# A hybrid decoder step on one core: the sampled-attention stage in another order, and two output tiles computed in pieces

## Chip, cores and metric

One Trainium2 chip, one core. The metric is device time in microseconds (us) of one execution. The kernel before took 1250.9 us (median of three runs, 1247.67 to 1252.53).

## The reference, cut to what matters

The kernel runs one step of a two-layer decoder for 512 prompt tokens and 8 sampled requests of 4 tokens each (32 sampled tokens), `D_MODEL` 1024. Layer 0 projects its input, runs a causal convolution on one half (LayerNorm, then `silu`) and attention with a forget gate on the other, and multiplies the concatenation with `w_out`. The sampled tokens attend to 256 cached rows in pages of 128, found by a page table, and to their own new rows:

```
y = jax.nn.silu(layer_norm(out, ln_g, ln_b))                      # conv branch
k_all = jnp.concatenate([gather_pages(cache_k[e], page_table), k], axis=1)
v_all = jnp.concatenate([gather_pages(cache_v[e], page_table), v], axis=1)
att = fox_attend(q, k_all, v_all, f_all[:, past_len:], f_all, q_pos_s, k_pos_s)
merged = jnp.concatenate([a_out, att.reshape(*att.shape[:2], D_B)], axis=-1)
xs = xs + merged @ wo
```

A squared-ReLU MLP (hidden 4096) follows in each layer; layer 1 has a spatial-gating unit in the place of attention.

## The kernel before, in words

Activations lie feature-major: `xT[128, 8, 544]`, tokens in the columns (32 sampled, then 512 prompt), 8 blocks of 128 features. Every dense product is made from three fp32r products: operands are split into a high part (ScalarE, `_hi`) and the rest (VectorE, `_lo`), and TensorE adds hi·hi, lo·hi and hi·lo into PSUM (`ps`, 8 banks of 512). One output tile (`tile`, L789) is 8 blocks k × 3 products × 2 halves of 272 columns, 48 matmuls, into a pair of banks. Weights come in blocks of 256 columns through `w_raw` (SyncE's queue) and are split by `split_hi` and `split_lo`.

Each engine has its own instruction list, written out by hand and joined by semaphores; an engine works strictly in its own order. Around the change, in layer 0:

- **Prompt attention** runs through 32 items (head, query block): scores and transposed probabilities on TensorE, maximum and normalisation on VectorE, exponent on ScalarE. The convolution's taps fill VectorE between them; the LayerNorm's variance is summed by TensorE (`channel_sums`, L999) after item 30. `pair_hi`/`pair_lo` write the attention result into `A_hi`/`A_lo`, blocks 4 to 7.
- **Sampled stage.** For each of 8 requests, `turn_pages(b)` (L1074) transposes the two pages of keys, 8 transposes into two banks; ScalarE copies one bank and VectorE the other to `kc_T` (`page_copy`). A slot of `kc_T` is used again by request b+4, so the copies of requests 4 to 7 wait for the first four requests' scores. `sample_scores(g)` for a group of four requests first adds the terms that need no page (forget sums, mask, own keys; L1087 to L1094), then the 32 products with the pages (L1100). Then `sample_max`, `sample_exp`, `sample_share`, `turn_sample` (three transposes), `sample_copy`, `sample_new_values` (L1123), `sample_values` (L1133), `own_heads`, `turn_values` (L1141), `gather_heads` (L2113), `sampled_lo`, which writes the 32 sampled columns of `A_hi`/`A_lo`, blocks 4 to 7.
- In the same stretch ScalarE takes the LayerNorm's square root, VectorE inverts it in four quarters (L2088) and scales `c_f` (L2090), ScalarE applies `Silu` (L1574) and rounds to `A_hi`, blocks 0 to 3 (L1579), VectorE writes `A_lo` (L2126) and splits the first three output tiles' weights (L1804). The `Silu` part stands after both groups' scores, since `q_bd`, `kn_T`, `nf_T` and `self_q` lie in the bytes of `A_hi`, blocks 0 to 3.
- **Output projection:** eight tiles (L800). Tile j is added to `xT` by VectorE (`add_to_x`, L2135); then ScalarE and VectorE prepare that block as an operand of the MLP (`to_ffn`): a series of roundings and subtractions per tile, the split of the next weights, sums of squares, and from the third tile on the weight sums of the first products of the MLP. Tile j+2 may start when tile j has been added.
- **MLP:** blocks are multiplied by a seven-product scheme in the order `ORDER` (L1213). The first six products of a chunk are p1, p5, p1, p5, p2, p2; the next, p6, waits for `part_11` (L2253), a reduction by VectorE.
- **Queues.** SyncE issues, in order: keys of requests 0 to 2, values of 0 to 3, keys of 3 to 7 (from request 5 on each after the transposes of request b-5), values of 4 to 7 (after the transposes of requests 3, 4, 6, 7), then the last two blocks of `w_out`, then the MLP's weights. GpSimd loads `w_spatial` and `b_spatial` after the first output tile.

Of the kernel before, what the change touches and what calls it, by code (L numbers as in the profile page):

```python
# [24 lines left out]
F32 = mybir.dt.float32  # L25
# [59 lines left out]
def build(nc, i, o):  # L85
# [78 lines left out]
    with ExitStack() as ctx:  # L164
# [104 lines left out]
        q_bd = at("q_bd", [P, PAIRS, NB, HQ], F32, reg1)  # L269
        kn_T = at("kn_T", [P, PAIRS, NS], F32, reg1 + 4096)  # L270
        nf_T = at("nf_T", [H * NB, KS], F32, reg1 + 4608)
        self_q = at("self_q", [H * NB, 2, P], F32, reg1 + 5760)
        assert 6784 <= CT * TB
        kc_T = [at(f"kc_T{s}", [P, PAIRS, NEWC], F32, reg2 + 4096 * s) for s in range(4)]
# [50 lines left out]
        MIX_BANK, MIX_BANK_S = (2, 4, 5), (3, 6, 7)  # L325
        X_BANK = (0, 2, 6)
# [307 lines left out]
        def _(pool):  # L634
# [103 lines left out]
            pool.memset(q_bd[:, :, :, :], 0.0).then_inc(bd_zero, 1)  # L738
# [50 lines left out]
        def _(pe):  # L789
            def tile(j, n, hi, lo, first_waits=None, k0=0, kn=KT):  # L790
# [3 lines left out]
                s = j % 2  # L794
# [283 lines left out]
            def sample_scores(g):  # L1078
# [14 lines left out]
                for p2 in range(PAIRS):  # L1093
                    pe.matmul(out[:, NEWC:KS], q_bd[:, p2, 4 * g:4 * g + 4, :].rearrange("p b c -> p (b c)"), kn_T[:, p2, :],  # L1094
                              start=False, stop=False, skip_group_check=True)
                for g_ in range(PAGES):
                    pe.wait_ge(kcT_evac[g_], 4 * g + 4)
                for p2 in range(PAIRS):
                    for b4 in range(4):
                        mm = pe.matmul(out[HQ * b4:HQ * b4 + HQ, 0:NEWC], q_bd[:, p2, 4 * g + b4, :],  # L1100
                                       kc_T[b4][:, p2, :], start=False, stop=(p2 == PAIRS - 1), skip_group_check=True)
                mm.then_inc(sc_done, 1)

            def turn_sample(g):
                pe.wait_ge(sp_ready, g + 1)
                out = ps[:, 2, :]
                if g == 0:
                    pe.wait_ge(kcT_evac[0], NB)
# [6 lines left out]
            def sample_new_values(g):  # L1115

                pe.wait_ge(spT_evac, g + 1)
                if g == 0:
                    for g_ in range(PAGES):
                        pe.wait_ge(kcT_evac[g_], NB)  # L1120
                else:
                    pe.wait_ge(root_done, 1)
                pe.matmul(ps[:, 5 + g, :], p_sT[0:NS, g, 2, :], v_nat[0:NS, 0, :], start=True, stop=False,  # L1123
                          skip_group_check=True)

            def sample_values(g):
# [3 lines left out]
                for u in range(PAGES):  # L1130
                    for b4 in range(4):
                        c = HQ * b4
                        mm = pe.matmul(ps[c:c + HQ, 5 + g, :], p_sT[:, g, u, c:c + HQ], v_pg[4 * g + b4][:, u, :],  # L1133
# [3 lines left out]
            def turn_values(g):  # L1137

                pe.wait_ge(own_done, g + 1)
                for p2 in range(PAIRS):  # L1140
                    mm = pe.transpose(ps[:, 3 + g, P * p2:P * p2 + P], own[:, g, P * p2:P * p2 + P], ident[:, :])  # L1141
# [12 lines left out]
            sample_new_values(1)  # L1154
            sample_values(1)
            turn_values(0)


            def merged_ready(k):
                if k == 2:  # L1160
                    turn_values(1)
                if k < CT:
                    pe.wait_ge(cyo_done, k + 1)
                else:
                    pe.wait_ge(ml_done, PAIRS + 2)

            pe.wait_ge(spT_evac, 2)
            for j in range(8):
                tile(j, N_OUT + j, A_hi, A_lo, merged_ready if j == 0 else None)
# [160 lines left out]
        def _(act):  # L1330
# [144 lines left out]
            def sample_prep(h):  # L1475

                rows_ = slice(HD * (h % 2), HD * (h % 2) + HD)
                act.activation(q_bd[rows_, h // 2, :, NQ * h:NQ * h + NQ],
# [46 lines left out]
            for s in range(FIRST_ALONE, H * QT):  # L1525
                item_slot(s)
                if 12 <= s < 12 + H:
                    if s == 12:
                        act.wait_ge(bd_zero, 1)
                    sample_prep(s - 12)  # L1530
# [907 lines left out]
```

## Time and profile before

| | |
|---|---|
| median of three runs | 1250.9 us |
| profiled execution, its own time | 1246.93 us |
| its span in the trace | 1245.2 us |
| busy: TensorE / VectorE / ScalarE / GpSimd | 96% / 69% / 49% / 5% |
| chain that ended last: TensorE / VectorE / ScalarE | 86% / 7% / 3% |
| granted TensorE clock, mean | 0.99 |

The profiled execution's time stands 1.73 us above its span. Busy shares are of the whole span; the stage at hand is some 40 us of it, from 250 to 290 us. A window view gives busy time per stretch, a timeline the instructions in order with the idle time before each and what ended it. The granted clock (PEclk) is a share of full speed: 1.00 stands for 2.4 GHz, 0.50 for 1.2 GHz.

### The profile page before, as it was taken

The page shows a single profiled execution, that of the slowest core. Times are in us where ns is not written, and L with a number is a line of the kernel's source. Part 1 is how long each engine was busy: PE and PEld are TensorE (multiplying, and loading weights), DVE is VectorE, ACT ScalarE, POOL GpSimd, SP SyncE. Part 2 cuts the span into 40 slices and gives each one's busy share as a digit, 9 for nine tenths or more (in the row PEclk, how much of TensorE's full clock was granted, in tenths as well). Part 3 has the DMA queues.
Part 4 walks back from the last instruction along what each step waited for, and adds up shares of the span by engine and source line. Part 5 has one row for each costly group of instructions (what it writes and reads, how often), then busy time and mean ns, then how long its engine had stood idle before and what let it go on. Part 6 is the DMA issues. An engine that isn't in the chain of part 4 may idle for free.

```text
span 1245.2 us, 23181 instructions
## 1 busy us (share of the span) xinstructions
PE 1199.5 (96%) x9394; PEld 1158.6 (93%) x9394; DVE 856.1 (69%) x1416; ACT 604.3 (49%) x1174; POOL 64.9 (5%) x111
## 2 busy tenths in 40 slices
PE   6999998889999999999999999989999999999998
PEld 5999886658999999999999999989999999999998
DVE  5798888656895685684686635678965855856852
ACT  5636644634564264273374424635652652642641
POOL 4010300000000000000000031030000000000000
PEclk9999997989999999999999999999999999999999
DMA  5431321344134143143142123222241251341312
GB/s 160 105 99 57 90 99 37 102 153 136 35 100 138 34 137 102 38 158 109 41 132 68 44 93 102 68 73 69 68 157 47 70 169 35 101 137 35 131 40 73
DMA packets 111777, 113.41 MB, mean 91 GB/s; under 512 B 6430, under 2 KB 105898, under 8 KB 111663
## 3 DMA queue, kind: packets, MB, share of 16 engines
q1 hardware_dynamic: 110111, 107.50, 26.7%
q0 software_dynamic: 1472, 4.41, 1.1%
q8 instruction: 75, 1.23, 0.4%
q14 instruction: 31, 0.25, 0.1%
q10 hardware_dynamic: 88, 0.02, 0.0%
HBM read 107.18 MB, written 5.16 MB: 90 GB/s over the span
## 4 chain that ended last, share of the span: by engine, by line
PE 86%; DVE 7%; ACT 3%; issue 2%; DMA 1%; POOL 1%; SPq 0%; ACTq 0%; DVEq 0%
PE ps L1237 31%; PE ps L1213 26%; PE ps L800 18%; PE ps L1039 5%; PE ps L952 1%; DMA w_raw<-in_w_in_ab 1%; DVE c_f L1893 1%; PE ps L982 1%; PE ps L999 1%; POOL A_lo L774 1%; PE ps L964 1%; DVE a_f L2411 1%; DVE w_lo L2174 1%; DVE w_lo L1804 0%; PE ps L1100 0%
## 5 line engine op out<-in xcount | busy, mean ns | idle before, releaser
L1597 ACT ACTIVATE w_hi<-w_raw 128x512 fp32r<-128x512 f32 x320 | 197.5, 626 | 236.8 <-PE ps L1237 177.7
L2174 DVE TENSOR_TENSOR w_lo<-w_raw,w_hi 128x512 fp32r<-128x512 f32 x320 | 214.3, 684 | 11.0 <-ACT w_hi L1597 10.9
L1237 PE MATMUL ps<-A_hi,w_hi 128*128 128x272 f32 x1024 | 212.4, 289 | 0.0
L1237 PE MATMUL ps<-A_lo,w_hi 128*128 128x272 f32 x1024 | 212.1, 289 | 0.0
L1237 PE MATMUL ps<-A_hi,w_lo 128*128 128x272 f32 x1024 | 211.3, 288 | 0.0
L1237 PEld LDWEIGHTS ps<-A_hi,w_hi 128*128 128x128 f32 x1024 | 161.0, 188 | 0.1
L1237 PEld LDWEIGHTS ps<-A_hi,w_lo 128*128 128x128 f32 x1024 | 161.0, 189 | 0.0
L2333 DVE TENSOR_TENSOR t_f<-ps,r_all 128x544 f32<-128x544 f32 x64 | 46.3, 724 | 166.3 <-PE ps L1237 166.3
L1237 PEld LDWEIGHTS ps<-A_lo,w_hi 128*128 128x128 f32 x1024 | 159.9, 189 | 0.0
L1213 PE MATMUL ps<-B_lo,w_hi 128*128 128x272 f32 x512 | 147.8, 289 | 0.0
L1213 PE MATMUL ps<-B_hi,w_lo 128*128 128x272 f32 x512 | 147.6, 288 | 0.0
L1213 PE MATMUL ps<-B_hi,w_hi 128*128 128x272 f32 x512 | 147.5, 288 | 0.0
L1213 PE MATMUL ps<-t_h,w_hi 128*128 128x272 f32 x384 | 111.7, 291 | 3.4 <-DVE w_lo L2174 3.4
L1213 PE MATMUL ps<-t_l,w_hi 128*128 128x272 f32 x384 | 111.3, 290 | 0.0
L1213 PE MATMUL ps<-t_h,w_lo 128*128 128x272 f32 x384 | 110.6, 288 | 0.0
L1213 PEld LDWEIGHTS ps<-B_hi,w_lo 128*128 128x128 f32 x512 | 96.5, 188 | 0.0
L1213 PEld LDWEIGHTS ps<-B_hi,w_hi 128*128 128x128 f32 x512 | 96.5, 188 | 0.0
L1213 PEld LDWEIGHTS ps<-B_lo,w_hi 128*128 128x128 f32 x512 | 96.4, 188 | 0.0
L800 PE MATMUL ps<-A_hi,w_hi 128*128 128x272 f32 x384 | 81.7, 294 | 8.2 <-DVE xT L1836 3.9
L1893 DVE SCALAR_TENSOR_TENSOR c_f<-glu_p,conv_wT,c_f 128x512 f32<-128x512 f32 x120 | 83.4, 741 | 0.2
L800 PE MATMUL ps<-A_lo,w_hi 128*128 128x272 f32 x384 | 80.6, 292 | 0.0
L800 PE MATMUL ps<-A_hi,w_lo 128*128 128x272 f32 x384 | 80.4, 291 | 0.0
(328 smaller groups left out, 2417.3 us busy)
## 6 DMA issues: line engine op xcount, KB each, us to landing
w_raw<-in_w_ff_up SPq DMA_DIRECT2D x64, 512.0 KB, 4.7
w_raw<-in_w_ff_down SPq DMA_DIRECT2D x64, 512.0 KB, 5.3
w_raw<-in_w_in_ab SPq DMA_DIRECT2D x20, 512.0 KB, 4.7
w_raw<-in_w_in_c SPq DMA_DIRECT2D x16, 512.0 KB, 4.4
w_raw<-in_w_out_ab SPq DMA_DIRECT2D x8, 512.0 KB, 4.8
k_pg<-in_cache_k SPq DMA_DIRECT2D x16, 256.0 KB, 4.6
v_pg<-in_cache_v SPq DMA_DIRECT2D x16, 256.0 KB, 3.8
w_raw<-in_w_out_c SPq DMA_DIRECT2D x8, 512.0 KB, 4.4
```

The lines of the kernel that those rows point to most:

```text
L774: pool.tensor_tensor(A_lo[:, k, :], a_f[:, k % 2, :], A_hi[:, k, :].bitcast(F32), ALU.subtract)\
L800: mm = pe.matmul(ps[:, 2 * s + half, 0:HALF], wt[:, j % 4, k, :], mv[:, k, half * HALF:(half + 1) * HALF], start=(k == 0 and at_ == 0), st ...
L952: pe.matmul(ps[:, bank, 0:n], qT[0:HD + 2, h, NS + P * q:NS + P * q + P], kT[0:HD + 2, h, NS:NS + n], start=True, stop=False, skip_group_c ...
L964: mm = pe.transpose(ps[:, 4 + s % 2, P * j:P * j + P], prob[:, s % 3, P * j:P * j + P], ident[:, :])
L982: mm = pe.matmul(ps[HD * even:HD * even + HD, 7, P * q:P * q + P], v_nat[:, 1 + j, HD * h:HD * h + HD], pT[(2 * t + even) % 6][:, P * j:P ...
L1039: mm = pe.matmul(nat_ps(m), mv[:, k, c0:c0 + P], wt[:, s:s + 2, k, :], start=(k == 0 and at_ == 0), stop=(k == KT - 1 and at_ == 2))
L1213: mm = pe.matmul(ps[:, product_bank((name, u)), 0:HALF], wt[:, k, :], mv[:, k, :], start=(name in ("p1", "p2", "p5") and k == 0 and at_ == 0),
L1237: mm = pe.matmul(down_banks(u)[:, half, :], wt[:, k % KH, :], mv[:, k, half * HALF:(half + 1) * HALF], start=(k == 0 and at_ == 0), stop=( ...
L1597: act.activation(ring(w_hi, q), half_source(q), ACT.Copy).then_inc(fh_done, 1)
L1893: dve.scalar_tensor_tensor(out=c_f[:, c, NS:T], in0=glu_p[:, c, tap:tap + S], scalar=conv_wT[:, c, tap:tap + 1], in1=c_f[:, c, NS:T], op0= ...
L2174: dve.tensor_tensor(ring(w_lo, q), half_source(q), ring(w_hi, q).bitcast(F32), ALU.subtract)\
L2333: dve.tensor_tensor(two(t1_f[:, 1, :]), down_banks(j), two(r_all[:, :]), ALU.mult).then_inc(dn_evac, 1)
```

## The change

On TensorE, `sample_scores` becomes `sample_biases` (the terms without pages) and `sample_keys`; the biases are placed between pages, the keys of group 0 after page 4. Output tiles 0 and 1 are cut into `out_part` pieces and placed between the steps of the sampled values; the half of columns 272 to 543 (without sampled tokens) is closed first. Bank pairs of the eight tiles follow `OUT_PAIR`; the other PSUM banks move with them (turned probabilities to 7, sampled values to 4 and 5, turned values to 6 and 7). `q_bd` moves into the prompt columns of `qT`, heads 0 and 1, and `self_q`, `nf_T`, `kn_T` into `nat_buf`, so `A_hi` is free earlier; `kc_T` is moved accordingly. GpSimd's clearing of `q_bd` waits for the scores of heads 0 and 1 too, VectorE's `forget_rows` (at item 10) for the stores of keys, ScalarE's `sample_prep` (from item 12 on) for `forget_rows`.

```diff
TensorE
-            for b in range(6):
-                turn_pages(b)
-            sample_scores(0)
+            def out_part(j, ks, halves):
+                n = N_OUT + j
+                if ks[0] == 0:
+                    pe.wait_ge(lo_done, n + 1)
+                    if j == 0:
+                        pe.wait_ge(kcT_evac[0], NB)
+                    else:
+                        pe.wait_ge(sexp_done, 2)
+                for k in ks:
+                    if k < CT:
+                        pe.wait_ge(cyo_done, k + 1)
+                    else:
+                        pe.wait_ge(ml_done, PAIRS + 2 if 0 in halves else PAIRS)
...
+            turn_pages(0)
+            turn_pages(1)
+            sample_biases(0)
+            turn_pages(2)
+            turn_pages(3)
+            sample_biases(1)
+            turn_pages(4)
+            sample_keys(0)
+            turn_pages(5)
             turn_pages(6)
             turn_pages(7)
-            sample_scores(1)
+            sample_keys(1)
+            out_part(0, range(0, CT), (0, 1))
             turn_sample(0)
+            out_part(0, range(CT, KT), (1,))
+            turn_sample(1)
             sample_new_values(0)
             sample_values(0)
-            turn_sample(1)
             sample_new_values(1)
             sample_values(1)
+            out_part(1, range(0, 1), (0, 1))
             turn_values(0)
...
+            out_part(1, range(1, 3), (0, 1))
+            turn_values(1)
+            out_part(1, range(3, CT), (0, 1))
+            out_part(1, range(CT, KT), (1,))
+            out_part(0, range(CT, KT), (0,))
+            out_part(1, range(CT, KT), (0,))
+            pe.wait_ge(ats_ok, 2)
+            for j in range(2, 8):
+                tile(j, N_OUT + j, A_hi, A_lo)
ScalarE
+                if s == H * QT - 2:
+                    act.activation(soft[:, 3, 0:1], eps[:, 0:1], ACT.Sqrt)
+            act.wait_ge(var_done, 1)
+            act.activation(two(r_all[:, :]), ps[:, 0:2, 0:HALF], ACT.Sqrt, bias=eps[:, 1:2], scale=1.0 / DA)\
+               .then_inc(root_done, 1)
             pair_hi(PAIRS - 1)
...
+            page_copy(0)
+            page_copy(1)
+            act.activation(soft[:, 3, 1:2], eps[:, 0:1], ACT.Silu)
+            page_copy(2)
+            page_copy(3)
+            smooth(0)
+            smooth(1)
+            for b in range(4, NB):
+                page_copy(b)
+            smooth(2)
+            smooth(3)
+            sample_exp(0)
+            sample_exp(1)
+            sample_copy(0)
+            sample_copy(1)
VectorE
+            for n in range(N_OUT, N_OUT + 3):
+                split_lo(n, n)
+            dve.wait_ge(root_done, 1)
+            link(dve.reciprocal(r_all[:, 0:T // 4], r_all[:, 0:T // 4]))
             pair_lo(PAIRS - 1)
...
+            for b in range(4):
                 page_copy(b)
...
+                if b < 3:
+                    invert_quarter(b + 1)
+            for c in range(CT):
+                dve.tensor_tensor(c_f[:, c, :], c_f[:, c, :], r_all[:, :], ALU.mult).then_inc(normed, 1)
+            page_copy(4)
+            page_copy(5)
+            smooth_lo(0)
+            page_copy(6)
+            smooth_lo(1)
+            page_copy(7)
+            sample_max(0)
+            smooth_lo(2)
             sample_max(1)
+            smooth_lo(3)
+            sample_share(0)
             sample_share(1)
```

`smooth(c)` is the `Silu` and the rounding of block c, `smooth_lo(c)` its rest; before, the three splits, the quarters and the scalings stood between the page copies, and `A_lo` of blocks 0 to 3 after `own_heads(0)`.

## Rows read from the trace of the kernel before

**Rows 1.** Windows: busy us of PE, PEld, DVE, ACT, POOL, PEclk, DMA, GB/s

```profile
250.44:260.15 9.71, 6.21 (x51) 5.15 (x49) 8.19 (x10) 4.76 (x7) 0.00 (x0) 1.00 0.70 239
260.15:267.73 7.58, 7.49 (x50) 4.93 (x49) 1.49 (x2) 0.00 (x0) 0.00 (x0) 0.55 0.11 43
267.73:289.59 21.86, 17.61 (x140) 10.85 (x140) 14.10 (x32) 12.82 (x24) 0.00 (x0) 1.00 0.30 97
289.59:343.90 54.31, 54.31 (x432) 54.23 (x432) 43.45 (x78) 28.82 (x53) 2.47 (x7) 1.00 0.29 98
343.90:345.74 1.84, 0.14 (x3) 0.03 (x1) 1.84 (x4) 0.63 (x1) 0.00 (x0) 1.00 0.00 0
```

**Rows 2.** Timeline of TensorE: start, length, operation, count, [idle before, releaser]

```profile
252.02 1.94 PE L1074 MATMUL ps<-ident,k_pg 128*128 128x128 f32 x16 [0.49 <-DVE A_lo L1989]
...
271.11 0.75 PE L1087 MATMUL ps<-nf_T,sel 64*128 64x288 f32 x2
...
273.55 1.93 PE L1100 MATMUL ps<-kc_T,q_bd 128*32 128x256 f32 x32
...
276.67 1.12 PE L1123 MATMUL ps<-v_nat,p_sT 32*128 32x512 f32 x2 [0.70 <-ACT p_sT L1553]
...
279.57 0.33 PE L1111 MATMUL ps<-ident,prob_s 128*128 128x128 f32 x1
```

**Rows 3.** Operations of VectorE, 250.4 to 289.6: count, busy us, mean ns, idle

```profile
L2076 DVE COPY kc_T<-ps 128x512 f32<-128x512 f32 x8 | 5.5, 684 | 6.8 <-PE ps L1100 6.1 <-PE ps L1074 0.7
...
L1804 DVE TENSOR_TENSOR w_lo<-w_raw,w_hi 128x1024 fp32r<-128x1024 f32 x4 | 4.9, 1224 | 0.1
...
L2088 DVE RECIPROCAL r_all<-r_all 128x136 f32<-128x136 f32 x4 | 4.0, 995 | 0.1
...
L2126 DVE TENSOR_TENSOR A_lo<-c_f,A_hi 128x544 fp32r<-128x544 f32 x4 | 2.9, 724 | 3.0 <-ACT A_hi L1579 3.0
...
L2113 DVE TENSOR_REDUCE at_s<-ps 128x16 f32<-128x128 f32 x8 | 1.8, 281 | 0.0
```

**Rows 4.** Timeline of ScalarE in the sampled stage

```profile
268.87 1.28 ACT L1547 ACT_TABLE_LOAD   x1
...
281.14 0.82 ACT L1574 ACTIVATE c_f<-c_f,vec 128x544 f32<-128x544 f32 x1
```

**Rows 5.** Timelines of GpSimd and VectorE: last store of keys, `self_q`

```profile
159.22 0.75 POOL L725 DMA_DIRECT2D out_k_prompt<-nat_buf  x1 [2.30 <-DVE nat_buf L1969]
...
205.33 0.47 DVE L2000 TENSOR_TENSOR self_q<-ps,sel 64x128 f32<-64x128 f32 x2
```

**Rows 6.** The page's DMA issues: count, KB each, us to landing

```profile
k_pg<-in_cache_k SPq DMA_DIRECT2D x16, 256.0 KB, 4.6
```

**Rows 7.** Timeline of VectorE: the additions to `xT`, and the first reduction

```profile
292.90 0.72 DVE L2135 TENSOR_TENSOR xT<-ps,xT 128x544 f32<-128x544 f32 x1 [2.23 <-PE ps L800]
...
298.91 0.72 DVE L2135 TENSOR_TENSOR xT<-ps,xT 128x544 f32<-128x544 f32 x1 [0.52 <-PE ps L800]
...
304.92 0.72 DVE L2135 TENSOR_TENSOR xT<-ps,xT 128x544 f32<-128x544 f32 x1 [0.62 <-PE ps L800]
...
316.95 0.72 DVE L2135 TENSOR_TENSOR xT<-ps,xT 128x544 f32<-128x544 f32 x1 [0.37 <-PE ps L800]
...
328.98 0.72 DVE L2135 TENSOR_TENSOR xT<-ps,xT 128x544 f32<-128x544 f32 x1 [0.24 <-PE ps L800]
...
344.92 0.71 DVE L2253 TENSOR_REDUCE t_f<-ps 128x272 f32<-128x544 f32 x1
```

**Rows 8.** Timeline of TensorE: the restart in the first feed-forward layer

```profile
345.74 0.36 PE L1213 MATMUL ps<-t_h,w_hi 128*128 128x272 f32 x1 [1.70 <-DVE w_lo L2174]
```

**Rows 9.** Timeline of TensorE near the kernel's start

```profile
22.04 0.82 PE L800 MATMUL ps<-A_hi,w_hi 128*128 128x272 f32 x2 [3.87 <-DVE xT L1836]
...
25.30 0.41 PE L800 MATMUL ps<-A_hi,w_lo 128*128 128x272 f32 x2
```

**Rows 10.** A stretch of the attention stage, columns as in rows 1

```profile
202.70:216.30 13.60, 10.86 (x47) 6.57 (x45) 11.15 (x29) 6.28 (x22) 0.00 (x0) 0.50 0.01 4
```

More of the change, by code:

```diff
@@ L268, in build @@
         gate = at("gate", [H, 4, T], F32, zone_kT + 12288)
[L269 to L274, printed above, removed]
+        q_all = at("q_all", [P, 2, T], F32, reg2)
+        q_bd = [q_all[:, p2 // 2, NS + NB * HQ * (p2 % 2):NS + NB * HQ * (p2 % 2) + NB * HQ].rearrange("p (b c) -> p b c", b=NB)
+                for p2 in range(PAIRS)]
+        self_q = at("self_q", [H * NB, 2, P], F32, zone_nb)
+        nf_T = at("nf_T", [H * NB, KS], F32, zone_nb + 1024)
+        kn_T = at("kn_T", [P, PAIRS, NS], F32, zone_nb + 2176)
+        assert 2688 <= 3 * 4 * 4 * (HD + 2) and 2 * TB <= 5120
+        kc_T = [at(f"kc_T{s}", [P, PAIRS, NEWC], F32, reg2 + (4096 * s + 5120 if s < 3 else 2 * KT * TB - 6144))
+                for s in range(4)]
         K_SLOTS = (zone_t, zone_t + 4096, zone_gs, zone_glu, zone_glu + 4096)
@@ L1117, in sample_new_values @@
                 pe.wait_ge(spT_evac, g + 1)
[L1118 to L1123, printed above, removed]
+                pe.wait_ge(kcT_evac[1], NB - 1 + g)
+                pe.matmul(ps[:, 4 + g, :], p_sT[0:NS, g, 2, :], v_nat[0:NS, 0, :], start=True, stop=False,
                           skip_group_check=True)
@@ L1139, in turn_values @@
                 pe.wait_ge(own_done, g + 1)
+                if g == 1:
+                    pe.wait_ge(spT_evac, 2)
                 for p2 in range(PAIRS):
-                    mm = pe.transpose(ps[:, 3 + g, P * p2:P * p2 + P], own[:, g, P * p2:P * p2 + P], ident[:, :])
+                    mm = pe.transpose(ps[:, 6 + g, P * p2:P * p2 + P], own[:, g, P * p2:P * p2 + P], ident[:, :])
                 mm.then_inc(own_T, 1)
-            for b in range(6):
-                turn_pages(b)
-            sample_scores(0)
+            def out_part(j, ks, halves):
[11 more added lines that the diff above has]
+                        pe.wait_ge(ml_done, PAIRS + 2 if 0 in halves else PAIRS)
+                    for wt, mv, at_ in ((w_hi, A_hi, 0), (w_lo, A_hi, 1), (w_hi, A_lo, 2)):
+                        for half in halves:
+                            mm = pe.matmul(ps[:, 2 * OUT_PAIR[j] + half, 0:HALF], wt[:, j % 4, k, :],
+                                           mv[:, k, half * HALF:(half + 1) * HALF],
+                                           start=(k == 0 and at_ == 0), stop=(k == KT - 1 and at_ == 2),
+                                           skip_group_check=True)
+                if ks[-1] == KT - 1 and 0 in halves:
+                    mm.then_inc(tile_done, 1)
@@ L2123, in _ @@
             own_heads(0)
-            for c in range(CT):
-                dve.wait_ge(cyh_done, c + 1)
-                dve.tensor_tensor(A_lo[:, c, :], c_f[:, c, :], A_hi[:, c, :].bitcast(F32), ALU.subtract).then_inc(cyo_done, 1)
             own_heads(1)
```

90 lines of the change are left out of this document (30 added, 60 removed).

## The prediction

> **What bounds the kernel now.** I began with the busy shares: TensorE has 96% of the span, so time can only be won where it waits, and where it runs at half clock. The table of windows [rows 1] shows where. From 250.44 to 260.15 us it is busy for 6.21 of 9.71 us; from 260.15 to 267.73 it is busy, but at a granted clock of 0.55; from 267.73 to 289.59 it stands still for 4.25 us more. Then 432 matmuls follow in 54.31 us without a gap, 0.126 us each. One more gap comes after them, 1.84 us before 345.74, in which VectorE is busy all the time. So there are two places: the sampled stage, and the entry to the MLP.
>
> The timeline of TensorE gives the stage's prices at full clock [rows 2]: 16 transposes in 1.94 us, so 0.11 us each and 0.9 us per request; the terms without pages from 271.11 to 273.55, 2.44 us; 32 products with pages 1.9 us; new and cached values of a group from 276.67 to 279.57, 2.90 us. Three turned pieces cost 0.4 us at the transposes' pace, a block of an output tile 6 × 0.126 = 0.75 us [rows 1]. The first group did the same terms and products in the window at 0.55, in 7.58 us in place of 4.35: half clock cost 3.2 us [rows 1, 2].
>
> The second view is VectorE's timeline after the stage [rows 7]. Between its first addition at 292.90 and the end of the reduction at 345.63 it waits for TensorE only four times: 0.52, 0.62, 0.37 and 0.24 us, 1.75 us in all. So the 52.7 us are a chain of VectorE's (with ScalarE's roundings in it), not of TensorE's. The product p6 needs that reduction, and TensorE's restart at 345.74 is that wait [rows 8] (the row names the split just before, which stands on the same list).
>
> **The stage, step by step.** Page 1 still starts at 252.02, after `A_lo` [rows 2]. What is put before it is covered: the square root and its table load fall in ScalarE's wait for the last probabilities, the three splits and one quarter of the inverse in VectorE's wait for `pair_hi`. Uncovered, they would put on the path about 2 us of ScalarE (a load of 1.28 us and a root priced like a `Silu`, 0.82 us [rows 4]) or 4.7 us of VectorE (three splits of 1.22 and a quarter of 1.00 [rows 3]).
>
> TensorE's new list, at the prices above: page 1 to 252.9; terms of group 0 to 255.4; pages 2 and 3 to 257.2; terms of group 1 to 259.65; page 4 to 260.55; products of group 0 to 262.4; pages 5 to 7 to 265.1. The terms cover the copies on which the pages used to wait. VectorE's four copies, three quarters and four scalings of c, 8.6 us at most at 0.68, 1.00 and 0.72 us (the last from the rests, which have the scalings' shape [rows 3]), fit between 251.9 and 261.4. From 262.4 it makes four copies and two rests of 0.72 us, with hardly a wait: the last copy ends at about 266.7, and TensorE waits 1.6 us. Products of group 1 to 268.7; four blocks of tile 0 to 271.7.
>
> Under them runs what used to stand on the path: ScalarE ends the fourth `Silu` (0.82 us [rows 4], its rounding counted the same at most) at 268.4, loads the `Exp` table (1.28 us [rows 4]) and has both exponents by 270.9. VectorE's shares are ready by then. So: turned probabilities 0 to 272.1, four half blocks (12 matmuls, 1.5 us) to 273.6, turned probabilities 1 to 274.0, values of both groups to 279.8. One block, turned values 0, two blocks, turned values 1, one block, with 0.45 us for each turning: 283.7. Half of tile 1 to 285.2, tile 0's other half to 286.7. The sampled columns go through VectorE and ScalarE meanwhile, four reductions of 0.28 us per group [rows 3], a rounding and a rest of 64 columns, under 1.6 us. The second group's start at 283 and are ready by 284.6, 0.6 us before they are needed; without that cover, 3 us of them would stand on the path.
>
> Tile 0 is added at about 287.0 in place of 292.90, and tile 1 is complete at 288.3, about 10.5 us earlier than now. In terms: 7.8 us of waits before 289.59, less 2.1 that stay (0.5 and 1.6), 3.2 us of half clock, and 1.6 us for the drain of the last matmul before each of some ten waits, which the records count as busy.
>
> **What reaches the end.** TensorE is 10.5 us ahead, but VectorE's chain begins only with tile 0, 5.9 us earlier, and it needs its 52.7 us less the 1.75 us of waits that now fall away [rows 7]: 287.0 + 51.0 + 0.1 = 338.1, against 345.74. **The gain at the restart is 7.6 us**, and behind it TensorE has no gap in which to lose it. TensorE, six products past its tiles, gets there at 333.5: its gap grows from 1.7 to about 4.5 us. What is late next is thus VectorE's list.
>
> A longer gap has a price that rows of the same kind show. After a gap of 3.87 us at the kernel's start, dense matmuls go at half pace: seven pairs from 22.04 to 25.30 take 3.26 us, where seven at 0.25 take 1.75, so 1.5 us lost [rows 9]. The gap of 1.70 us cost nothing: the clock stayed at 1.00 [rows 1, 8]. A gap of 4.5 is nearer to the first, so I take 1.5; the ends are 0 and the 3.2 us above. The Trainium skill, page "TensorE: Matmul & The Clock Gate", section "HAM oscillation — how this bites in real kernels", says that a long idle stretch between bursts sends the engine back to half rate. By that rule the gain is 6.1, by the row of the short gap alone 7.6.
>
> **Edits with no price of their own.** The bank moves change no instruction. VectorE's wait for stored keys at item 10 has scores and ScalarE's exponents behind it, but the last store was issued at 159.22, and `self_q` is written at 205.33 [rows 5]. ScalarE's wait at item 12 adds nothing: its exponent of item 14, ahead of it, already depends on `self_q` through item 14's scores. GpSimd's clearing of `q_bd` waits for eight items' scores, which TensorE issues before the projections that it waited for already. SyncE's gathers follow the transposes: request 7's keys are issued 2.5 us later, at 256.5, and land by the median of 4.6 us [rows 6] at 261 to 262, before 264.2; values 5 come later too, values 6 and 7 and the third weight block about 5 us earlier, at 264 to 266.5, 10 us before use. The fourth weight block, the MLP's first block and GpSimd's two loads move forward 4 to 6 us together, as close to one another as now. Were a key page late after all, every us would go onto the path.
>
> **Sum.** The profiled execution took 1246.93 us: 1246.93 - 7.6 + 1.5 = 1240.8. The median of the runs is 0.32% above that execution; in its measure the forecast is 1244.8 us. About 0.5%, 6.3 us, can be told from no change here.
>
> **Rivals.**
> - *The clock holds at the gap.* For it: the short gap; against it: rows 9. Gain 7.6, 1243.3 us.
> - *The clock falls among the pages as well.* In 250.44 to 260.15 TensorE did nothing but transposes and waits, at 1.00, and only then fell [rows 1]. The new order mixes in matmuls, but has its longest wait, 1.6 us, behind three pages of transposes. Price 3.2 us on the path: gain 2.9, 1248.0 us. The Trainium skill's same page, section "Part 4: PE-mode transpose", says that transposes do not count as busy for the clock. By that rule this is the likelier case; the trace, with 9.7 us of them at 1.00, agrees in part at best.
> - *TensorE's lead is kept whole.* VectorE's chain would have to be shorter than its rows, by hidden waits in it: gain 10.5 less 1.5 at most, up to 10.5 without the drop, 1240.4 us. Against it: VectorE's full windows before 345.74.
> - *Slower: the clock falls among the pages and stays down.* In the attention stage it stayed at 0.50 for 13.6 us [rows 10], with work as sparse as the sampled one. Here it would cost half of that, 6.8, and the later drop 1.5: 8.3 against 7.6, 0.7 us slower, 1251.6 us. It turns slower from 12.2 us at half clock on; over the whole stage, 31 us, it would be near 1260.
> - *The early table loads do not do what they are for*: `Silu`'s load stands on the path again, 1.28 us [rows 4]. Gain 4.8, 1246.1 us.
>
> **How the numbers follow.** Forecast 0.47; clock holds 0.20; clock falls among the pages 0.13; lead kept 0.08; slower 0.06; table loads 0.06. The forecast's gain of 6.1 lies at the edge of 0.5%; its unknowns (0 to 3.2 for the drop, about 1 us for the start of the chain) split it evenly. Faster: half of the forecast, nearly all of the clock that holds, the lead kept: 0.47. Slower by over 0.5% is the long half clock alone: 0.03. The rest, 0.50, lies within. The range goes from the lead kept, 1240, to the fall among the pages with the runs' own scatter, 1249; only the slower case and parts of the outer ones lie outside.
>
> **What would show it.** Right: page 7's copy is the only long wait in 252 to 288; the first addition to `xT` at about 287; four waits of VectorE gone from the additions; a gap of 4 to 5 us on TensorE that ends about 7.6 us earlier than 345.74 with `part_11`; then a granted clock of 0.5 for about 3 us. Wrong: a clock under 1.00 between 255 and 285, a wait of a page for its gather, a first addition later than 289, or an MLP that starts over 9 us earlier.

## The result and the profile after

| | before | after |
|---|---|---|
| median of the runs | 1248.56 us (8 runs, 1246.22 to 1252.53) | 1242.02 us (8 runs, 1237.76 to 1243.86) |
| ratio after to before | | 0.9943, 95% interval 0.9928 to 0.9958 |
| profiled execution: time, span | 1246.93, 1245.2 us | 1243.86, 1242.2 us |
| page 0 to the first addition to `xT` | 42.46 us | 36.66 us |
| page 0 to product p6 | 95.30 us | 87.41 us |
| gap of TensorE ahead of p6, first layer | 1.70 us | 4.08 us |
| p6 to the first finished block (`d0`) | 42.85 us | 44.37 us |

The change makes the kernel 6.5 us faster by the medians, 0.57%; forecast were 6.1 us. A second set of runs of the same kernel gave 1240.53 us and a ratio of 0.9935 (0.9914 to 0.9955).

The two profiled spans differ by only 3.0 us, because the profiled execution of after comes to page 0 at 253.89 us in place of 250.44. These 3.45 us arise ahead of page 0 and not in the sampled stage: the first scores of the prompt attention are already 1.45 us late (165.74 against 164.29 us), and in the attention stage TensorE's clock is lower for longer (mean granted clock from 195 to 235 us 0.79 against 0.83). Over all executions profiled in this study, of either kernel and its variants, page 0 starts between 248.9 and 253.9 us. So the stages are compared from page 0 on, and never by the spans.

First the table of windows of after, with stretches that answer to [rows 1]: page 0 to the score terms, to the first piece of tile 0, to the last piece, to the last product ahead of p6, the gap, and what follows it.

```profile
core 0: us, PE busy (x) PEld busy (x) DVE busy (x) ACT busy (x) POOL busy (x), PEclk, DMA share, GB/s
253.89:263.60 9.71, 9.15 (x74) 8.25 (x73) 7.92 (x12) 5.07 (x8) 0.00 (x0) 1.00 0.57 163
263.60:272.17 8.57, 7.01 (x93) 4.88 (x91) 6.12 (x11) 7.72 (x13) 0.00 (x0) 1.00 0.71 232
272.17:291.87 19.70, 19.70 (x151) 15.08 (x148) 7.53 (x20) 4.11 (x12) 0.75 (x1) 1.00 0.26 86
291.87:337.20 45.33, 45.33 (x362) 45.12 (x360) 39.03 (x72) 27.26 (x52) 1.72 (x7) 1.00 0.31 106
337.20:341.30 4.10, 0.01 (x1) 0.03 (x1) 4.10 (x8) 1.53 (x3) 0.00 (x0) 1.00 0.00 0
341.30:345.00 3.70, 3.70 (x18) 3.70 (x19) 2.40 (x5) 0.91 (x2) 0.00 (x0) 0.57 0.55 177
```

From 253.89 to 337.20 us the granted clock is 1.00 throughout, where [rows 1] had 0.55 for 7.58 us. TensorE is busy for 16.16 of the first 18.28 us, and from 272.17 on it makes 513 matmuls in 65 us without a gap. Then it stands still for 4.10 us in which VectorE is busy all the time, and the 3.70 us behind that go at 0.57. From here to the end, half clock costs 1.5 us more than before (p6 to `d0`: 44.37 against 42.85).

The timeline of TensorE through the stage:

```profile
255.54 1.06 PE L1079 MATMUL ps<-ident,k_pg 128*128 128x128 f32 x8 [0.56 <-DVE A_lo L2028]
...
270.31 1.93 PE L1109 MATMUL ps<-kc_T,q_all 128*32 128x256 f32 x32 [1.56 <-DVE kc_T L2121]
...
272.17 0.52 PE L1165 MATMUL ps<-A_hi,w_hi 128*128 128x272 f32 x2
...
275.27 0.27 PE L1118 MATMUL ps<-ident,prob_s 128*128 128x128 f32 x1
```

These answer to [rows 2]. Page 1 waits as it did. The only long wait among pages is that of group 1's products for page 7's copy, 1.56 us. The first piece of tile 0 starts 1.86 us later, and from there on no row has an idle time in front.

VectorE's additions and its first reduction, which answer to [rows 7], and TensorE's restart, [rows 8]:

```profile
290.55 0.72 DVE L2184 TENSOR_TENSOR xT<-ps,xT 128x544 f32<-128x544 f32 x1 [1.20 <-PE ps L1165]
...
295.96 0.72 DVE L2184 TENSOR_TENSOR xT<-ps,xT 128x544 f32<-128x544 f32 x1
...
301.27 0.72 DVE L2184 TENSOR_TENSOR xT<-ps,xT 128x544 f32<-128x544 f32 x1
...
312.83 0.72 DVE L2184 TENSOR_TENSOR xT<-ps,xT 128x544 f32<-128x544 f32 x1
...
324.54 0.72 DVE L2184 TENSOR_TENSOR xT<-ps,xT 128x544 f32<-128x544 f32 x1
...
331.24 0.72 DVE L2184 TENSOR_TENSOR xT<-ps,xT 128x544 f32<-128x544 f32 x1
...
340.47 0.72 DVE L2302 TENSOR_REDUCE t_f<-ps 128x272 f32<-128x544 f32 x1
```

```profile
341.30 0.36 PE L1246 MATMUL ps<-t_h,w_hi 128*128 128x272 f32 x1 [4.08 <-DVE w_lo L2223]
```

The first addition waits for TensorE; no later one does. From 290.55 to the end of the reduction VectorE takes 50.64 us, against 52.7 before. The longer gap ahead of p6 is what the change leaves to TensorE: it is early, and VectorE's list is not.

### The profile page after: what moved, and what is told of

The parts are those of the page before. It is cut to its first block, busy times and chain, and to the rows that moved or that the text cites. A ratio compares the mean times of both kernels' runs of the same rounds, so it can differ in the third digit from the quotient of the medians.

```text
span 1242.2 us, 23180 instructions
## 1 busy us (share of the span) xinstructions
PE 1199.2 (97%) x9394; PEld 1160.6 (93%) x9394; DVE 855.9 (69%) x1416; ACT 605.3 (49%) x1176; POOL 64.9 (5%) x111
## 4 chain that ended last, share of the span: by engine, by line
PE 85%; DVE 8%; ACT 3%; issue 1%; DMA 1%; POOL 1%; SPq 0%; ACTq 0%; DVEq 0%
PE ps L1270 31%; PE ps L1246 26%; PE ps L805 15%; PE ps L1044 5%; PE ps L957 1%; DMA w_raw<-in_w_in_ab 1%; PE ps L1165 1%; DVE w_lo L1843 1%; PE ps L987 1%; DVE c_f L1932 1%; DVE w_lo L2223 1%; PE ps L1004 1%; PE ps L969 1%; POOL A_lo L779 1%; DVE a_f L2460 1%
## 5 line engine op out<-in xcount | busy, mean ns | idle before, releaser
L1270 PE MATMUL ps<-A_hi,w_hi 128*128 128x272 f32 x1024 | 212.2, 288 | 0.0
L1270 PE MATMUL ps<-A_lo,w_hi 128*128 128x272 f32 x1024 | 212.0, 288 | 0.0
L1270 PE MATMUL ps<-A_hi,w_lo 128*128 128x272 f32 x1024 | 211.2, 288 | 0.0
L805 PE MATMUL ps<-A_hi,w_hi 128*128 128x272 f32 x352 | 75.4, 296 | 8.2 <-DVE xT L1875 4.3
L1246 PEld LDWEIGHTS ps<-t_h,w_hi 128*128 128x128 f32 x384 | 73.0, 190 | 6.3 <-DVE w_lo L2223 6.2
L805 PE MATMUL ps<-A_lo,w_hi 128*128 128x272 f32 x352 | 74.1, 292 | 0.0
```

The costliest lines, as they stand in the source:

```text
L805: mm = pe.matmul(ps[:, 2 * s + half, 0:HALF], wt[:, j % 4, k, :], mv[:, k, half * HALF:(half + 1) * HALF], start=(k == 0 and at_ == 0), st ...
L1246: mm = pe.matmul(ps[:, product_bank((name, u)), 0:HALF], wt[:, k, :], mv[:, k, :], start=(name in ("p1", "p2", "p5") and k == 0 and at_ == 0),
L1270: mm = pe.matmul(down_banks(u)[:, half, :], wt[:, k % KH, :], mv[:, k, half * HALF:(half + 1) * HALF], start=(k == 0 and at_ == 0), stop=( ...
```

## The experiments

All profiles were read in the same three stretches, so that the early part of an execution does not enter. Page 0 is TensorE's first transpose of a key page, the first addition is VectorE's first `add_to_x`, and `d0` stands for the first finished block of the feed-forward layer, read at the start of VectorE's first addition `xT<-t_f,xT`. The runs were made in sets, each beside its own runs of the kernel before: their median was 1249.92 us beside `after_5`, `early_sums`, `fill_gap` and `tile0_only`, and 1247.30 us beside the others. So across sets the ratios are compared, not the medians.

| kernel | page 0 to first addition | page 0 to p6 | p6 to `d0` | median, us | ratio to before, 95% |
|---|---|---|---|---|---|
| before | 42.46 | 95.30 | 42.85 | 1248.56 | |
| `early_sums_before` | 43.44 | 94.42 | 43.36 | 1244.54 | 0.9969 (0.9957 to 0.9981) |
| `pages_only` | 37.68 | 90.53 | 42.86 | 1242.11 | 0.9956 (0.9940 to 0.9972) |
| `tile0_only` | 36.17 | 89.02 | 42.86 | 1241.32 | 0.9946 (0.9927 to 0.9965) |
| after, first profile | 36.66 | 87.41 | 44.37 | 1242.02 | 0.9943 (0.9928 to 0.9958) |
| `after_5` | 36.71 | 87.46 | 45.48 | 1240.53 | 0.9935 (0.9914 to 0.9955) |
| `after_look1` | 36.71 | 87.47 | 44.39 | 1241.18, one run | |
| `after_look2` | 36.71 | 87.48 | 44.24 | 1238.41, one run | |
| `no_early_tables` | 37.92 | 88.69 | 45.21 | 1243.35 | 0.9968 (0.9956 to 0.9979) |
| `fill_gap` | 36.71 | 87.44 | 42.86 | 1238.07 | 0.9935 (0.9913 to 0.9958) |
| `early_sums` | 36.65 | 83.73 | 43.85 | 1235.81 | 0.9906 (0.9888 to 0.9925) |
| `earlier_sums` | 36.67 | 83.76 | 44.36 | 1236.86 | 0.9904 (0.9888 to 0.9921) |

**The yardstick.** `after_5` is the changed kernel, run again beside the first experiments.

> The changed kernel itself, unaltered, as the measure for the others of this set. Expected: 6 to 7 us below the kernel before (ratio 0.9943 so far), with a gap of TensorE of about 4.1 us ahead of product p6 of the first feed-forward layer and about 1.4 us lost at half pace behind it. If the earlier comparison had owed its gain to one lucky set of runs, the difference would come out under 4 us.

Measured: 1240.53 us, ratio 0.9935 (0.9914 to 0.9955), a gap of 4.10 us ahead of p6 and a clock of 0.50 in the 5.8 us behind it. The gain holds. Its runs lie around 1238 us at a mean clock of 0.994 and around 1242.3 at 0.989, and those of the kernel before beside it around 1246 us at 0.991 and 1250 at 0.987. Hence the wide intervals, and hence the reading of stages rather than of totals below.

**What sets the restart.** `early_sums` takes two reductions forward in VectorE's list.

```diff
                 for u in range(TAIL):
+                    if c == 0 and u < 2:
+                        part_11(layer, c, u)
                     up_round(layer, c, *ORDER[u])
                     if u < TAIL - 1:
                         weights_lo(q0 + u + RING - 1)
...
-                if (name == "p2" and u < 2) or (name == "p1" and u >= 2):
+                if (name == "p2" and u < 2 and c > 0) or (name == "p1" and u >= 2):
                     part_11(layer, c, u)
```

> Only the first two reductions of each feed-forward layer's first chunk (part_11 of 0 and 1) stand earlier in VectorE's list: ahead of the split of weights 7 and of weights 8, instead of four splits later. Theory (VectorE's list, not TensorE, sets the restart at 341.30): part_11(0) runs at about 336.8, the gap of 4.08 us shrinks to about 0.4, the clock stays at 1.00 and the 1.44 us behind it are not lost; in the second layer the gap of 1.70 goes too: 3.7 + 1.4 + 1.7 = 6.8 us below the changed kernel. Rival (another wait takes its place: the rests that p6 and p7 need, or weights split too late): TensorE stops again within the next four products, and under 2.5 us are won. Rival (TensorE loses it later, to VectorE's list in the same chunk): the restart comes early but the second chunk starts at the same time as now.

VectorE's timeline in it (last addition and three reductions), and TensorE's two waits:

```profile
329.78 0.72 DVE L2184 TENSOR_TENSOR xT<-ps,xT 128x544 f32<-128x544 f32 x1
...
335.36 0.72 DVE L2302 TENSOR_REDUCE t_f<-ps 128x272 f32<-128x544 f32 x1
...
337.20 0.71 DVE L2302 TENSOR_REDUCE t_f<-ps 128x272 f32<-128x544 f32 x1
...
343.28 0.72 DVE L2310 TENSOR_REDUCE t_f<-ps 128x272 f32<-128x544 f32 x1
```

```profile
336.18 0.37 PE L1246 MATMUL ps<-t_h,w_hi 128*128 128x272 f32 x1 [0.44 <-issue]
...
344.10 0.36 PE L1246 MATMUL ps<-t_h,w_hi 128*128 128x272 f32 x1 [0.35 <-issue]
```

Measured: the reduction starts 5.6 us after the last addition to `xT`, which is at 329.78 (9.2 us in after: 331.24, 340.47). TensorE waits 0.44 us in place of 4.08, p6 comes 83.73 us after page 0, so 3.68 us earlier, and the clock stays at 1.00. So VectorE's list sets the restart, and nothing that p6 itself needs is late behind it. But p6 to `d0` takes 43.85 us in place of the 42.86 that full clock allows: 1.0 us is given back, of which the second wait, 0.35 us ahead of p4, is a part. In the second layer p6 to the end takes 364.0 in place of 363.6 us. The run is 4.7 us below `after_5`, not 6.8: the theory's mechanism holds, and a part of the rival that VectorE's list takes some of it back.

**The same two lines in the kernel before.**

> The kernel before with the same two reductions moved forward as in early_sums. Theory (before the change TensorE was only 1.7 us ahead of VectorE, so there is no more to win): the gap of 1.70 us ahead of p6 closes in both layers, of which the first chunk takes back up to 1 us each time as in early_sums; 1.5 to 3.4 us below the kernel before. early_sums lies 8 to 11 us below this one: TensorE's whole lead out of the change (10.5 by the forecast's count) is seen once VectorE's list is out of its way. Rival (the earlier reductions are worth the same wherever they stand, 2 to 4 us): early_sums lies 6 to 7 us below this one, as the changed kernel lies below the kernel before.

The first addition and the first reduction in VectorE's timeline:

```profile
293.28 0.72 DVE L2135 TENSOR_TENSOR xT<-ps,xT 128x544 f32<-128x544 f32 x1 [2.23 <-PE ps L800]
...
342.94 0.72 DVE L2253 TENSOR_REDUCE t_f<-ps 128x272 f32<-128x544 f32 x1 [1.20 <-PE ps L1213]
```

VectorE now waits 1.20 us for TensorE ahead of the reduction: in the kernel before, TensorE is the later one as soon as the list is put right. Its restart is 94.42 us after page 0, 0.9 us earlier than before; the first addition is 1.0 us later in this execution, whose clock was down to 0.60 from 258 us on already, where that of [rows 1] held until 260; so 1.9 us belong to the edit. `early_sums` restarts 10.7 us earlier than this one, or 9.7 without that 1.0; the forecast counted TensorE's lead as 10.5. So the lead is there once VectorE's list lets it through. From page 0 to `d0` the edit is worth 138.15 - 137.78 + 1.0 = 1.4 us in the kernel before and 131.78 - 127.58 = 4.2 us in the changed one, and about 1.3 us more in the second layer in either. In whole runs the two kernels with the edit differ by 0.9969 - 0.9906 = 0.63%, 7.9 us, between the two theories; there the edit is worth 0.31% in the kernel before and 0.29% by the ratios in the changed one (4.7 us, 0.38%, by the medians). The runs alone can't tell 3 us from 5 here; that the edit is worth more after the change rests on the profiles, one of each kernel with the edit, and by the ratios it is not shown.

**One more reduction forward.** In `earlier_sums`, `part_22(0)` also comes forward.

```diff
                     if c == 0 and u < 2:
                         part_11(layer, c, u)
+                    if c == 0 and u == 6:
+                        part_22(layer, c, 0)
...
-                if name == "p7":
+                if name == "p7" and (c > 0 or u > 0):
                     part_22(layer, c, u)
```

> early_sums, and in addition the first reduction of the second row (part_22 of 0) of each layer's first chunk stands ahead of the split of weights 13 instead of after that of weights 14 and a sum of weights. In early_sums p6 started 83.7 us after page 0 (changed kernel 87.4), but 1.0 us of the 3.7 was given back within the next 8 us, where p4 waited for this reduction. Theory: the 1.0 us stays, in both layers, and the run is 1 to 2 us below early_sums. Rival (a split of weights is late in its place): the same time as early_sums.

Every row of TensorE's timeline between 335 and 366 us that has a wait in front:

```profile
336.34 0.36 PE L1246 MATMUL ps<-t_h,w_hi 128*128 128x272 f32 x1 [0.44 <-issue]
...
361.21 0.36 PE L1246 MATMUL ps<-t_h,w_hi 128*128 128x272 f32 x1 [0.72 <-DVE t_f L2302]
```

The wait ahead of p4 is gone, and the next pair's p6 waits 0.72 us instead. p6 to `d0` takes 44.36 us, longer than without the edit, and the whole run is the same (0.9904 against 0.9906). The rival holds. Behind the restart VectorE has no slack for some 25 us (busy for 24.4 of 24.9 us from 336.34 to 361.20, and for 24.8 of 24.8 in `early_sums`), and between these two orders the choice is only where TensorE waits.

**What the longer gap costs.** `fill_gap` puts 28 matmuls into it whose result nobody reads.

```diff
                         product(layer, c, *ORDER[u])
+                        if layer == 0 and c == 0 and ORDER[u] == ("p2", 1):
+                            for _ in range(28):
+                                pe.matmul(ps[:, 6, 0:HALF], B_hi[:, 0, 0:P], B_hi[:, 0, 0:HALF], start=True, stop=True)
```

> 28 matmuls of 272 columns, whose result nobody reads, stand on TensorE after product p2(1) of the first chunk of the first layer, in its gap of 4.08 us (28 x 0.127 = 3.6 us). Theory (the half pace behind the restart is the price of the standstill): p6 still starts at the same point of VectorE's list, the granted clock stays at 1.00, p6 and its followers run at 0.127 us each from the start, and the run is 1.4 us below the changed kernel. Rival (the half pace has another cause, such as operands that arrive late): p6 starts slowly all the same, no change. Rival (VectorE, not TensorE, sets the pace of the next products): full clock, but under 0.5 us won.

The timeline of TensorE, and the window from p6 on:

```profile
333.84 3.67 PE L1283 MATMUL ps<-B_hi 128*128 128x272 f32 x28
...
338.09 0.36 PE L1246 MATMUL ps<-t_h,w_hi 128*128 128x272 f32 x1 [0.59 <-issue]
```

```profile
338.09:342.00 3.91, 3.91 (x31) 3.91 (x32) 3.50 (x6) 1.52 (x4) 0.00 (x0) 1.00 0.57 186
```

p6 starts at the same point (87.44 us after page 0), now at 0.127 us per matmul from the start, and reaches `d0` in 42.86 us instead of 44.37: the 1.5 us at half clock are the price of the standstill. In whole runs this could not be told: the median is 2.5 us below that of `after_5`, but the ratios are equal.

Two more profiles of the unaltered kernel, one execution each, ask whether the fall happens every time.

> The changed kernel unaltered, one more profiled execution. Question: does the clock fall behind the gap of 4.1 us in every execution? Its times come in two groups, about 1238 us at a mean granted clock of 0.994 and about 1242.5 at 0.989; the two profiles so far are of the second group and show falls behind the gap and behind the waits near 820 us. Theory (each fall happens in some executions only): a profile of the first group shows a clock of 1.00 from the gap on, and product p6 to the first finished block in 42.9 us instead of 44.4. Rival (the fall behind this gap is always there, and the groups differ elsewhere): 44.4 us or more in either group.

> As after_look1, another execution: the same two expectations, 42.9 us from p6 to the first finished block at a mean clock of 0.994, or 44.4 us at any mean clock.

The gap and the stretch behind it in the second, whose mean clock was 0.994:

```profile
333.19:337.30 4.11, 0.01 (x1) 0.04 (x1) 4.11 (x8) 1.54 (x3) 0.00 (x0) 0.96 0.00 0
337.30:340.30 3.00, 3.00 (x13) 3.00 (x14) 2.33 (x4) 0.00 (x0) 0.00 (x0) 0.50 0.43 126
340.30:344.00 3.70, 3.70 (x31) 3.70 (x30) 1.81 (x3) 2.30 (x5) 0.00 (x0) 0.99 1.05 353
```

The rival holds. The clock falls behind this gap at a mean clock of 0.994 too; p6 to `d0` took 44.39 us in `after_look1` and 44.24 in `after_look2`. Over the five profiles with a gap of about 4.1 us, 1.4 to 2.6 us were lost (44.24 and, in `after_5`, 45.48, less 42.86). What `after_look2` lacks is another fall: near 820 us, where the first tile of the second layer's output projection waits for GpSimd three times, at last for 1.88 us, the clock fell in eight of the twelve profiles and held in four. From the last block of the first layer to p6 of the second, the kernel before, with the fall, takes 181.6 us, and `fill_gap`, without it, 180.0; the gap ahead of that p6 is 1.70 us in both. So this makes 1.6 us of the difference between executions. Two more parts stand in the twelve traces. The first scores of the prompt attention start between 164.1 and 166.0 us. From there to page 0 it takes 84.8 us in the five profiles with a mean granted clock of 0.87 from 195 to 235 us, 85.4 to 86.6 in the four with 0.83, and 87.1 to 88.2 in the three with 0.79. The kernel before shows 0.83 and, in `early_sums_before`, 0.87; the three with 0.79 are all of the changed kernel or a variant of it. Whether the change makes the longer stretch likelier can't be told from two profiles of the one side.

**The page order without the pieces.** `pages_only` keeps both tiles whole.

```diff
             sample_keys(1)
-            out_part(0, range(0, CT), (0, 1))
             turn_sample(0)
-            out_part(0, range(CT, KT), (1,))
-            turn_sample(1)
             sample_new_values(0)
             sample_values(0)
+            turn_sample(1)
...
+            for j in range(8):
+                if j == 2:
+                    pe.wait_ge(ats_ok, 2)
+                tile(j, N_OUT + j, A_hi, A_lo, merged_ready if j == 0 else None)
```

> The changed kernel's order of pages, score terms, Silu and shares, but both output tiles whole and after the sampled values, as in the kernel before. Theory (the page order and the pieces are two gains of about the same size): turned probabilities start 21 to 22 us after page 0 (before: 25.0), the rest of the stage takes its old 17.5 us to the first addition, so page 0 to first addition is 38.5 to 39.5 us (before 42.5, changed kernel 36.7); VectorE waits for TensorE four times in the additions as before; the gap ahead of p6 is 1.7 us again; 3 to 4 us below the kernel before, 3 to 4 above the changed one. Rival (the pieces alone make the gain, since TensorE's waits only move): within 1 us of the kernel before. Rival (the page order makes all of it): within 1 us of the changed kernel.

TensorE's timeline at group 1's products, the first turned probabilities and the cached values of both groups, then VectorE's at the first additions:

```profile
265.37 1.93 PE L1109 MATMUL ps<-kc_T,q_all 128*32 128x256 f32 x32 [1.55 <-DVE kc_T L2124]
...
269.40 0.33 PE L1118 MATMUL ps<-ident,prob_s 128*128 128x128 f32 x1 [2.10 <-DVE prob_s L2117]
...
271.96 3.23 PE L1136 MATMUL ps<-v_pg,p_sT 128*32 128x512 f32 x16
...
277.33 1.92 PE L1136 MATMUL ps<-v_pg,p_sT 128*32 128x512 f32 x16
```

```profile
286.62 0.72 DVE L2187 TENSOR_TENSOR xT<-ps,xT 128x544 f32<-128x544 f32 x1 [2.24 <-PE ps L805]
...
292.64 0.72 DVE L2187 TENSOR_TENSOR xT<-ps,xT 128x544 f32<-128x544 f32 x1 [0.52 <-PE ps L805]
...
298.65 0.72 DVE L2187 TENSOR_TENSOR xT<-ps,xT 128x544 f32<-128x544 f32 x1 [0.63 <-PE ps L805]
```

Page 0 to p6 takes 90.53 us: 4.8 of the 7.9 us come from the page order, 3.1 from the pieces on top of it (the pieces without the page order were not tried). The page order gives a little more than expected. The first addition comes 37.68 us after page 0, only 1.0 us later than with pieces, although the clock was 0.50 from 272 to 274 us here, behind the wait of 2.10 us for the shares, which tile 0's pieces fill in after. That half clock is itself a part of what the pieces save: in this profile group 0's cached values take 3.23 us where group 1's take 1.92, and its new values 1.46 where group 1's take 1.12, 1.65 us together. The rest of the pieces' part is in the additions, which wait 0.52 us and more for TensorE again, as in [rows 7]. The gap ahead of p6 is 1.7 us, and no clock is lost behind it; so from page 0 to `d0` the pieces are worth 133.39 - 131.78 = 1.6 us, and in whole runs 1.6 to 2.6 us by the ratios (0.9956 against 0.9943 and 0.9935), whose intervals overlap.

**Only tile 0 in pieces.**

```diff
             sample_values(1)
-            out_part(1, range(0, 1), (0, 1))
             turn_values(0)
-            out_part(1, range(1, 3), (0, 1))
             turn_values(1)
-            out_part(1, range(3, CT), (0, 1))
-            out_part(1, range(CT, KT), (1,))
             out_part(0, range(CT, KT), (0,))
-            out_part(1, range(CT, KT), (0,))
+            pe.wait_ge(sexp_done, 2)
+            tile(1, N_OUT + 1, A_hi, A_lo)
             pe.wait_ge(ats_ok, 2)
```

> The page order and tile 0 in pieces stay; tile 1 is one whole tile behind tile 0. TensorE has 6.1 us of dense work left instead of putting it into the sampled steps' waits. Theory (TensorE's lead beyond VectorE's chain buys nothing): tile 0 is added at about 289.7 to 290.6 on the clock of the changed kernel's profile, tile 1 is complete at about 295.8, when VectorE wants it (295.96 there); the next tiles make VectorE wait some 0.2 to 0.6 us each, at most 1 us in all; the gap ahead of p6 falls from 4.1 us to under 1.5, and the 1.4 us at half pace are not lost: 0 to 1.4 us below the changed kernel. Rival (TensorE's lead matters: pieces of tile 1 pay in full): 4 to 6 us above the changed kernel, at the kernel before or 2 us below it.

TensorE's timeline at tile 0's last piece and tile 1's start, then VectorE's additions to `xT` and the first reduction:

```profile
282.12 0.60 PE L1165 MATMUL ps<-A_hi,w_hi 128*128 128x272 f32 x1 [2.02 <-DVE A_lo L2169]
...
285.01 0.45 PE L805 MATMUL ps<-A_hi,w_hi 128*128 128x272 f32 x2
```

```profile
285.24 0.72 DVE L2181 TENSOR_TENSOR xT<-ps,xT 128x544 f32<-128x544 f32 x1 [2.04 <-PE ps L1165]
...
291.26 0.72 DVE L2181 TENSOR_TENSOR xT<-ps,xT 128x544 f32<-128x544 f32 x1 [0.52 <-PE ps L805]
...
297.28 0.72 DVE L2181 TENSOR_TENSOR xT<-ps,xT 128x544 f32<-128x544 f32 x1 [0.63 <-PE ps L805]
...
309.30 0.72 DVE L2181 TENSOR_TENSOR xT<-ps,xT 128x544 f32<-128x544 f32 x1 [0.37 <-PE ps L805]
...
321.33 0.72 DVE L2181 TENSOR_TENSOR xT<-ps,xT 128x544 f32<-128x544 f32 x1 [0.23 <-PE ps L805]
...
337.28 0.71 DVE L2299 TENSOR_REDUCE t_f<-ps 128x272 f32<-128x544 f32 x1
```

Tile 0 is added 0.5 us sooner than in after (36.17 us), but the four waits of [rows 7] are back, to a hundredth, and p6 comes 1.6 us later (89.02). Tile 1's pieces thus bring 1.6 us at the restart, not nothing, as the theory had it. Most of that is again clock: behind the wait of 2.02 us, which tile 1's pieces fill in after, the granted clock is 0.50 (from 283 to 285 us), and the 12 matmuls from 282.12 to 285.01 take 2.89 us where 12 at 0.126 would take 1.5. By this estimate 1.4 of the 1.6 us are the price of that fall, and the theory left it out; the profile is of one execution, so how often it happens is not known. The pieces cost 1.4 to 2.6 us behind it, since the gap grows from 1.7 to 4.1 us: from page 0 to `d0` the two differ by 131.88 - 131.78 = 0.1 us, and the runs by less than their intervals. So of what tile 1's pieces win, nothing can be seen at the end.

**The early table loads.**

```diff
-                if s == H * QT - 2:
-                    act.activation(soft[:, 3, 0:1], eps[:, 0:1], ACT.Sqrt)
...
-            act.activation(soft[:, 3, 1:2], eps[:, 0:1], ACT.Silu)
```

> The changed kernel without the two one-column activations that load the tables of Sqrt and Silu ahead of time. Theory: the load of Sqrt (1.28 us) falls between the last copied probabilities and the root, and delays pair_hi, A_lo and page 1 by 1.28 us; the load of Silu falls into ScalarE's wait of 2.03 us for the first scaled c and costs nothing if it is issued in that wait, or 1.28 us more if it comes behind it. 1.3 to 2.6 us above the changed kernel. Rival (both are covered by other waits): no change, within 0.5 us.

ScalarE's timeline, and TensorE's row of page 1:

```profile
249.19 1.28 ACT L1569 ACT_TABLE_LOAD   x1
...
258.56 1.28 ACT L1595 ACT_TABLE_LOAD   x1
...
260.57 0.84 ACT L1595 ACTIVATE c_f<-c_f,vec 128x544 f32<-128x544 f32 x1 [0.73 <-DVE c_f L2136]
```

```profile
253.11 1.06 PE L1079 MATMUL ps<-ident,k_pg 128*128 128x128 f32 x8 [1.76 <-DVE A_lo L2025]
```

The load of `Sqrt` now stands between the last copied probabilities and the root, and page 1 waits 1.76 us in place of 0.56: 1.2 us. The load of `Silu` is issued at 258.56, inside the wait for the first scaled c, and `Silu` still waits 0.73 us behind it: its early load is worth nothing. Page 0 to p6 grows by 1.28 us. By the ratios the runs lie 0.25 to 0.33% above the changed kernel, 3 to 4 us (0.9968 against 0.9943 and 0.9935), more than that. In the profile the clock's fall behind the gap is longer, too: p6 to `d0` takes 45.21 us in place of 44.37. It took 45.48 in `after_5`, whose tables are loaded early, so this is not put down to the edit; the rest of the difference in the runs stays open.

## Why the prediction was right

By its own steps, counted from page 0, which it put at 250.44:

- *The page order.* Forecast were the terms in the pages' waits, one wait of 1.6 us and the last values 29.4 us after page 0. Measured: 1.56 us, and values to 283.3, 29.4 us after page 0. `pages_only` shows it as a part of its own.
- *The first addition* at 36.6 us: 36.66. *VectorE's chain* of 51.0 us: 50.6. *The restart* 7.6 us earlier: 7.9. *TensorE's lead* of 10.5 us: 10.3, the 7.9 and the 2.4 by which the gap grew. That a reduction of VectorE's, not TensorE, sets it is shown by `early_sums` and by the full window of VectorE ahead of p6; that the four waits fall away only because tile 1 is early as well, by `tile0_only`. Not in the prediction is that the pieces also keep two falls of the clock out of the stage (1.65 us in `pages_only`, about 1.4 in `tile0_only`).
- *The gap* of 4.5 us: 4.08. *Half clock behind it*, 1.5 us (0 to 3.2), taken from [rows 9]: 1.51 in the profile of after and 1.4 to 2.6 over all five, so that the first profile agrees to a hundredth is luck. `fill_gap` shows that it is the gap's. The clock of 1.00 behind the gap of 1.70 us, which [rows 1] and [rows 8] do not reach, is borne out by p6 to `d0`, 42.85 us in the kernel before. The rival in which the clock holds at the gap, 0.20, was met in none of the five executions. The rule of the Trainium skill that the prediction named for this (page "TensorE: Matmul & The Clock Gate", section "HAM oscillation — how this bites in real kernels": a long idle stretch sends the engine back to half rate) agrees with all five.
- *Net*: 7.6 - 1.5 = 6.1 us; in the profiles 7.9 - 1.5 = 6.4, in the runs 6.5. The median forecast, 1244.8 us, lies 2.8 us above the measured 1242.02; 2.3 of these are its starting point, the median of three runs of the kernel before (1250.9), which is 1248.56 over eight. That the measured gain, 0.57%, comes out clear of no change had been put at about one half.
- *The clock among the pages.* The rival, 0.13, rested in part on the Trainium skill, same page, section "Part 4: PE-mode transpose", by which transposes do not count as busy for the clock in the same way. From page 0 to the gap the granted clock is 1.00 in all four profiles of the changed kernel, through three pages of transposes with a wait of 1.56 us behind them. By that rule alone a fall was to be expected there; the trace does not show one. Where a wait of 2.1 us (`pages_only`) or 2.0 (`tile0_only`) was left in the stage, the clock did fall.
- *Sqrt's and Silu's loads.* That rival was mis-sized: it put `Silu`'s load on the path at 1.28 us. Without early loads it is `Sqrt`'s that lies there, at 1.2 us, and `Silu`'s is covered either way. In the changed kernel both stand in waits, as the main case had it.
- *TensorE's lead kept whole* did not come about, as VectorE's list allows no more; `early_sums` and `early_sums_before` together show the lead once more, 9.7 to 10.7 us for 10.5.
- Not weighed beforehand: page 0 itself moves by 2 us and more between executions, and a comparison of the spans of one profile with one would have given 3 us.

Not tried: why the stretch at half clock in the attention stage, ahead of the change, is longer in one execution than in another.

## What to carry to other kernels

When an engine is brought ahead of another's list, look at what that list does just before the two meet: here a few lines that reorder VectorE's list, worth 1.4 us from page 0 to the first finished block in the kernel before, were worth 4.2 us on top of the change by the profiles (0.31% and 0.29% in whole runs, which do not show the difference), and the kernel with both (`early_sums`, 1235.81 us, 0.9906) is the fastest that was found, with `earlier_sums` its equal. A lead that ends in a longer standstill is paid for a second time in clock: tile 1's pieces won 1.6 us and lost 1.4 to 2.6. Compare stages from a common mark, with several profiles, before a difference of spans is read as an effect.

## What was not expected of the hardware

- Whether the clock falls behind a wait differs from execution to execution of the same order: behind the three waits near 820 us, the last of 1.88 us, it fell in eight of twelve profiles, at 1.6 us each. Behind the gaps of 1.7 us ahead of p6 it never did, and behind those of 4.1 us always.
- A filled gap kept the clock at 1.00 although the filling took 3.67 of the 4.25 us only: in this profile 0.59 us of standstill behind dense work cost nothing.
- ScalarE loaded a table ahead of an activation whose operand was not there yet: in `no_early_tables` `Silu`'s load ran at 258.56 to 259.84, and its operand came at 260.57.
